# Expert stage of a two-layer encoder: narrow experts on the even partitions, slots spread over all partitions, no remainders on GpSimd, the last k of gate and up multiplied whole in fp32

## The reference, cut to what matters

```python
xt = x.reshape(t, d)                       # t = 1024 tokens, d = 1024
g_idx = argmax of 4 group logits; top_p, top_e = the 2 best of the 8 experts of that group
gate = (g_w[:, None] * top_p).reshape(-1)  # 2048 pairs of token and expert, 32 experts
...
def expert_block(args):                    # for the tokens of one expert
    hid = jax.nn.silu(xe @ w1[e]) * (xe @ w3[e])   # w1, w3: 1024 x 512
    return hid @ w2[e]                             # w2: 512 x 1024
out = jax.ops.segment_sum(yb * buf_gate[:, None], buf_tok, num_segments=t)
```

## Time and profile before

| | us |
|---|---|
| median of 3 runs | 2560.96 (2559.26 to 2565.32) |
| profiled execution | 2557.62 |
| its span | 2555.8 |
| TensorE busy in the span | 2329.6 (91%) |
| VectorE busy | 1884.1 (74%) |
| ScalarE busy | 1474.9 (58%) |
| GpSimd busy | 883.5 (35%) |

### The profile page before, as it was taken

The page is one execution under the profiler, slowest core; times in us unless marked ns, Lnnn a source line. Parts: engine busy times, 40 slices in busy tenths (PEclk is TensorE's granted clock), DMA queues, the critical chain, the costliest instruction groups (busy, mean ns, idle before and its releaser), DMA issues. The chain is left out here.

```text
span 2555.8 us, 33503 instructions
## 1 busy us (share of the span) xinstructions
PE 2329.6 (91%) x11266; PEld 1803.8 (71%) x11266; DVE 1884.1 (74%) x2206; ACT 1474.9 (58%) x1814; POOL 883.5 (35%) x492
## 2 busy tenths in 40 slices
PE   8989999899998899999998999997998899999997
PEld 7768877587876666666666877875886666666664
DVE  7838856678379999899894141478678899899893
ACT  6438842322226888778874241277416777888782
POOL 0001100101003766767660000036003666767662
PEclk9989999999989999999999999998998999999999
DMA  5110001111358999999992031023338999999985
GB/s 182 42 59 2 2 21 66 74 33 38 116 201 337 370 380 375 376 382 379 381 350 81 30 111 67 33 51 116 136 125 349 361 392 387 382 378 374 370 337 208
DMA packets 91932, 540.28 MB, mean 211 GB/s; under 512 B 15596, under 2 KB 27533, under 8 KB 66742
## 3 DMA queue, kind: packets, MB, share of 16 engines
q1 hardware_dynamic: 73926, 499.84, 50.7%
q0 software_dynamic: 15168, 33.59, 5.2%
q10 hardware_dynamic: 2736, 5.51, 0.6%
HBM read 511.58 MB, written 47.22 MB: 219 GB/s over the span
## 5 line engine op out<-in xcount | busy, mean ns | idle before, releaser
L2664 DVE TENSOR_TENSOR wL_rest<-ring,wH 128x2048 fp32r<-128x2048 f32 x162 | 467.4, 2901 | 29.3 <-ACT wH L2563 29.3
L2563 ACT CAST wH<-ring 128x2048 fp32r<-128x2048 f32 x192 | 366.3, 1910 | 76.5 <-PE psum L2397 67.0
L2664 DVE TENSOR_TENSOR wL_rest<-xnT,wH 128x2048 fp32r<-128x2048 f32 x96 | 271.5, 2828 | 35.7 <-ACT wH L2563 35.7
L2389 PE MATMUL psum<-wH,xgH 128*128 128x512 f32 x544 | 221.5, 407 | 54.1 <-DVE xgL L2664 54.1
L2563 ACT CAST wH<-xnT 128x2048 fp32r<-128x2048 f32 x128 | 243.4, 1905 | 15.4 <-PE psum L2397 15.4
L2302 POOL TENSOR_TENSOR wL_rest<-ring,wH 128x2048 fp32r<-128x2048 f32 x30 | 197.9, 6596 | 88.8 <-ACT wH L2563 88.8
L2389 PE MATMUL psum<-wH,hidH 128*128 128x512 f32 (+1 forms) x512 | 207.1, 405 | 22.3 <-DVE hidL L2664 22.3
L2391 PE MATMUL psum<-wH,xgL 128*128 128x512 f32 x544 | 214.4, 394 | 0.0
L2391 PE MATMUL psum<-wH,hidL 128*128 128x512 f32 (+1 forms) x512 | 201.2, 393 | 0.0
L2302 POOL TENSOR_TENSOR wL_rest<-xnT,wH 128x2048 fp32r<-128x2048 f32 x32 | 148.3, 4635 | 129.6 <-ACT wH L2563 129.6
L2389 PEld LDWEIGHTS psum<-wH,xgH 128*128 128x128 f32 x544 | 103.2, 190 | 89.2 <-issue 43.6
(11 more groups left out here) (513 smaller groups left out, 5790.2 us busy)
## 6 DMA issues: line engine op xcount, KB each, us to landing
ring<-in_moe_w SPq DMA_DIRECT2D x92, 2048.0 KB
xnT<-in_moe_w SPq DMA_DIRECT2D x68, 2048.0 KB, 15.4
ow<-in_moe_w SPq DMA_DIRECT2D x34, 2048.0 KB, 14.2
ring<-in_ev_w_in SPq DMA_DIRECT2D x6, 2048.0 KB
ring<-in_od_w_in SPq DMA_DIRECT2D x6, 2048.0 KB
ring<-in_moe_w SPq DMA_DIRECT2D x16, 512.0 KB, 6.0
xn_scratch<-xn_route SPq DMA_DIRECT2D x14, 512.0 KB, 2.6
v_att<-in_x SPq DMA_DIRECT2D x8, 512.0 KB, 4.6
```

Of the source, the lines that this page charges most:

```text
L2389: nc.tensor.matmul(psum[rows, bank, :], xh[:, k, rows], w3[0][:, n, cols], start=(half == 0 and n == 0), stop=False)
L2563: nc.scalar.copy(half_of(wH, i, b, c, half), raw(i, b, c, half)).then_inc(w_high, 1)
L2664: return nc.vector.tensor_tensor(out, whole, high.bitcast(F32), ALU.subtract)
```

## The change

1. Narrow experts no longer use partitions 0 to 63 but the even ones of all 128. Gathers and adds have 128 partitions for every expert; the odd ones of a narrow expert have indices out of bounds. Its tokens are transposed like a wide one's, and the even columns are taken from the result. The table `turn_of_partition` spreads an expert's slots, wide or narrow, over all partitions.
2. GpSimd makes no remainders; VectorE makes all.
3. In the second half of gate and up, the last of the four k is not split: TensorE multiplies it whole in fp32, from the loaded weights and from unsplit tokens (xgW). Cast and remainder of these halves have 1536 columns instead of 2048.
4. The slot of such a tile is freed when TensorE has used it (w_used), since the whole product reads it.

```diff
-    half = np.arange(LESS)
-    turn_of_half = LESS // 4 * (half % 4) + half // 4
-    turn_of_partition = np.concatenate([turn_of_half, LESS + turn_of_half])
+    turn_of_partition = 16 * np.array([0, 4, 2, 6, 1, 5, 3, 7])[np.arange(P) % 8] + np.arange(P) // 8
...
-                def by_gpsimd(i, b, c, half):
-                    return c == 1 and half == 1 and not first(i, b)
+                def in_parts(i, b, c, half):
+                    last_out = isinstance(i, int) and i == PAIRS
+                    return 3 if c < 2 and half == 1 and not last_out else 4
...
                         def freed(i, b, c):
-                            if by_gpsimd(i, b, c, 1):
-                                sp.wait_ge(w_rest, rests(i, b, c, 0))
-                                sp.sem_inc(met, 1)
-                            wait_rest(sp, i, b, c, 1)
+                            if in_parts(i, b, c, 1) < 4:
+                                sp.wait_ge(w_used, after(i, b, c))
+                            else:
+                                sp.wait_ge(w_rest, rests(i, b, c, 1))
...
+                        def whole_product(bank, rows, i, b, c, half, ks):
+                            w = raw(i, b, c, half).rearrange("p (k c) -> p k c", k=len(ks))
+                            nc.tensor.matmul(psum[rows, bank, :], xgW[:, rows], w[:, len(ks) - 1, :],
+                                             start=False, stop=False)
...
-                            wait_rest(pe, i, b, c, half)
+                            if len(split_ks) < len(ks):
+                                whole_product(banks[0], slice(0, P), i, b, c, half, ks)
+                            pe.wait_ge(w_rest, rests(i, b, c, half))
...
-                            last = len(ks) - 1 if half else len(ks)
+                            last = len(split_ks) - 1 if half else len(split_ks)
                             for n in range(last):
                                 both_parts(n, False)
-                            wait_rest(pe, i, b, c, half)
-                            for n, k in enumerate(ks):
+                            if len(split_ks) < len(ks):
+                                whole_product(bank, S, i, b, c, half, ks)
+                            pe.wait_ge(w_rest, rests(i, b, c, half))
+                            for n, k in enumerate(split_ks):
...
-                                if small(i, b) and k == 0:
-                                    nc.tensor.transpose(psum[:, 0, 0:P], xg[:, b, 0:P], ident[:])
-                                elif small(i, b):
-                                    last = nc.tensor.transpose(psum[:, 0, k * LESS:(k + 1) * LESS],
-                                                               xg[S, b, k * P:(k + 1) * P], ident[S, S])
-                                else:
-                                    last = nc.tensor.transpose(psum[:, k // 4, (k % 4) * P:(k % 4 + 1) * P],
-                                                               xg[:, b, k * P:(k + 1) * P], ident[:])
+                                last = nc.tensor.transpose(psum[:, k // 4, (k % 4) * P:(k % 4 + 1) * P],
+                                                           xg[:, b, k * P:(k + 1) * P], ident[:])
...
+                    def even(a):
+                        return a.rearrange("p k (t two) -> p k t two", two=2)[:, :, :, 0]
+                    def even_x():
+                        return even(psum[:, 0:2, :].rearrange("p b (k t) -> p (b k) t", k=4))
...
                                 act.wait_ge(x_hi, e + 1)
-                                nc.scalar.copy(xgH[:, :, S], turned_small(0, KD)).then_inc(xh_ok, 1)
+                                nc.scalar.copy(xgW[:, S], even_x()[:, KD - 1, :])
+                                nc.scalar.copy(xgH[:, :, S], even_x()[:, 0:KD - 1, :]).then_inc(xh_ok, 1)
...
-                            if by_gpsimd(i, b, c, half):
-                                return
+                            cols = slice(0, 512 * in_parts(i, b, c, half))
                             dve.wait_ge(w_high, 2 * chunk(i, b, c) + half + 1)
...
-                                rest(hidL[:, :, S], turned_small(4, 4), hidH[:, :, S]).then_inc(hl_ok, 1)
+                                rest(even(hidL[:]), turned_hid(), even(hidH[:])).then_inc(hl_ok, 1)
```

More of the change, by code:

```diff
@@ L2062, in experts @@
                 idx = sb(st, "gidx" + nm, [P, 2], I32)
-                xgH = sb(st, "xgH" + nm, [P, KD, P], F32R)
-                xgL = sb(st, "xgL" + nm, [P, KD, P], F32R)
+                xgH = sb(st, "xgH" + nm, [P, KD - 1, P], F32R)
+                xgL = sb(st, "xgL" + nm, [P, KD - 1, P], F32R)
+                xgW = sb(st, "xgW" + nm, [P, P])
                 act_h = sb(st, "act_h" + nm, [P, DE])
@@ L2286, in fetch @@
                             e = 2 * i + b
-                            rows = S if small(i, b) else slice(0, P)
                             at = number(rank_of(i, b))
                             pool_e.wait_ge(x_hi, e - 1)
-                            nc.gpsimd.tensor_copy(idx[rows, b:b + 1], slots[rows, bass.ds(at, 1)]).then_inc(idx_ok, 1)
+                            nc.gpsimd.tensor_copy(idx[:, b:b + 1], slots[:, bass.ds(at, 1)]).then_inc(idx_ok, 1)
                             pool_e.wait_ge(idx_ok, e - 1)
@@ L2311, in give @@
                                 pool_e.wait_ge(given, gave + 16 * e)
-                            nc.gpsimd.tensor_copy(yidx[rows, b:b + 1], slots[rows, bass.ds(at, 1)]).then_inc(yidx_ok, 1)
+                            nc.gpsimd.tensor_copy(yidx[:, b:b + 1], slots[:, bass.ds(at, 1)]).then_inc(yidx_ok, 1)
                             pool_e.wait_ge(yidx_ok, e + 1)
@@ L2458, in gate @@
                                 else:
-                                    product((2 + c,), xgH, xgL, i, b, c, half, ks, slice(0, P))
+                                    product((2 + c,), xgH, xgL, i, b, c, half, ks)
                         def out(i, b, at_i, at_b, c):
@@ L2465, in out @@
                             for half in range(2):
-                                product((5, 6), hidH, hidL, at_i, at_b, c, half, range(2 * half, 2 * half + 2),
-                                        S if small(i, b) else slice(0, P))
+                                product((5, 6), hidH, hidL, at_i, at_b, c, half, range(2 * half, 2 * half + 2))
                         def one(i, b):
@@ L2562, in split @@
                                 act.wait_ge(w_used, q - 3)
-                            nc.scalar.copy(half_of(wH, i, b, c, half), raw(i, b, c, half)).then_inc(w_high, 1)
+                            cols = slice(0, 512 * in_parts(i, b, c, half))
+                            nc.scalar.copy(half_of(wH, i, b, c, half)[:, cols], raw(i, b, c, half)[:, cols]
+                                           ).then_inc(w_high, 1)
                         def move_x(i, b):
@@ L2572, in move_x @@
                                 act.wait_ge(turned, e + 1)
-                                nc.scalar.copy(xgH[:, 4 * half:4 * half + 4, :], quarter(half)).then_inc(xh_ok, 1)
+                                if half:
+                                    nc.scalar.copy(xgW[:], quarter(1)[:, 3, :])
+                                n = 4 - half
+                                nc.scalar.copy(xgH[:, 4 * half:4 * half + n, :], quarter(half)[:, 0:n, :]).then_inc(xh_ok, 1)
                         def store_y(i, b, at_i, at_b, c):
@@ L2612, in move_hid @@
                             if small(i, b):
-                                nc.scalar.copy(hidH[:, :, S], turned_small(4, 4)).then_inc(hh_ok, 1)
+                                nc.scalar.copy(even(hidH[:]), turned_hid()).then_inc(hh_ok, 1)
                             else:
@@ L2679, in move_x @@
                                 dve.wait_ge(xh_ok, turned_moves(i, b) + half + 1)
-                                ks = slice(4 * half, 4 * half + 4)
-                                ins = rest(xgL[:, ks, :], quarter(half), xgH[:, ks, :])
+                                n = 4 - half
+                                ks = slice(4 * half, 4 * half + n)
+                                ins = rest(xgL[:, ks, :], quarter(half)[:, 0:n, :], xgH[:, ks, :])
                             ins.then_inc(xl_ok, 1)
```

63 lines of the change are left out of this document (23 added, 40 removed).

## The result

The changed kernel takes 2539.16 us (median of 4, 2534.08 to 2542.4) beside 2560.11 of the kernel before (2556.65 to 2565.32): ratio 0.9915, interval 0.9891 to 0.9939. The forecast was 2542. The profiled execution took 2538.32, its span is 2536.5.

The account below looks back on a forecast made before the run. Bound: a loop of engines waiting for each other, 35.82 us a pair, not the weight stream. Pairs -10.7 and layer starts and ends -8 take 2560.96 to 2542 us; forecast band 2532 to 2552, range 2522 to 2564.

Parts of the forecast that it names:

- The waits: TensorE's three waits in the narrow stage: the first two go, the one for xgL stays at 1.1 us.
- Leg 1: Wide stage, first wide gate product to first narrow one: 18.05 us grows by 0.69 to 18.74.
- +0.25 to +0.3: Narrow expert's transposes on TensorE: eight full-size ones cost this many us more than one full and seven small.
- Leg 2: Narrow stage, first narrow gate product to next wide one: 17.77 us, the next wide gate starting 1.10 earlier.
- I take 0.875: Price in us of each 128x512 fp32 whole product on TensorE, taken from the overflow block's rows.
- Starts and ends of the layers: Outside the steady pairs: -2.5 us at each layer's start, -1.5 at its end, together -8.
- Costed at nothing: GpSimd's gathers and adds on 128 partitions, and strided reads and writes for narrow experts: no cost.
- SP's queue: Weight-load issues: four of six slots freed later, three by about 3 us, without moving the landings.
- the reserve is 24.9 - 16.0 = 8.9 us: Weight slots: 24.9 us from issue to cast, landing at most 16.0, so 8.9 us spare.
- Rival 1: Weight stream is the wall: pace stays near 35.8 us, only layer starts are won, 2556 us; chance 0.16.
- rival 3: More is won: better spread gather rows, TensorE's work the bound, 34.3 us a pair, 2514 us; chance 0.13.
- Rival 2: TensorE dearer: whole products cost 0.38 us more each, +0.73 net a pair, 2572 us; chance 0.15.

Follow-up runs that it names:

- experiments 8 and 9: Narrow whole product on 128 token columns (upper 64 zeros), in the changed kernel: 2531.26 us; in that kernel with VectorE's xgL moved ahead: 2483.38 us.
- Experiment 1: Changed kernel with narrow experts back in partitions 0 to 63 and the old slot table: 2549.62 us, ratio 0.9958.
- experiment 4: Kernel before the change, with one edit: VectorE makes all remainders, GpSimd none: 2528.57 us, ratio 0.9857.
- experiment 10: Changed kernel with VectorE's xgL ahead of gate remainder and multiplication, and narrow experts back in the lower 64 partitions: 2531.95 us, ratio 0.9877.
- experiment 2: Changed kernel without whole products, all k split, slots freed by the remainder: 2517.59 us, ratio 0.9832.
- experiment 3: Changed kernel, but GpSimd again makes the remainder of up's second half, with 1536 columns: 2539.01 us, ratio 0.9912.
- experiment 11: Changed kernel with whole products in wide experts only and VectorE's xgL ahead of gate remainder and multiplication: 2469.8 us, ratio 0.9641.
- experiment 5: Changed kernel without whole products, and with VectorE's xgL of the next expert ahead of gate remainder and multiplication: 2521.76 us, ratio 0.9836.
- experiment 12: Kernel of experiment 11 with VectorE's remainders of the wide halves on 2048 columns, the last 512 unread: 2544.22 us, ratio 0.9919.
- experiment 7: Changed kernel with VectorE's xgL of the next expert ahead of gate remainder and multiplication: 2494.26 us, ratio 0.973.

## Why the prediction was right, and where its steps were not

The time (2542 against 2539.16) and the pace (35.41 against 35.33) came as forecast, in part by luck: errors in the steps cancelled. By its steps:

- *The waits.* Two of three went and xgL's stayed, 1.20 against "stays at 1.1". VectorE took over both remainders at 2.29 and 1.74 us. Right.
- *Leg 1.* Forecast 18.74, measured 18.40. The wide whole products cost what was said (988.73 to 990.29, 1.56 us less 3 x 0.227 = 0.88). The term that was too big is "+0.25 to +0.3" for the narrow expert's transposes: from their start to the next product they take 997.36 - 996.57 = 0.79 us, and before it was 997.72 - 996.94 = 0.78. One full transpose and seven small ones had no smaller price than eight full ones.
- *Leg 2.* Forecast 16.67, measured 16.93. The term that was too small is the narrow whole product, "I take 0.875": 1.16. It was taken from rows with 128 columns of tokens, and 64 cost more (experiments 8 and 9). The one in the narrow gate stands in the chain that ends in xgL: 0.28 us more there, 0.26 in the leg. ScalarE's copy after the narrow gate starts 4.57 us after the gate's first product (1007.48 - 1002.91), 3.87 before, +0.70 where +0.42 was forecast.
- *Starts and ends of the layers.* Forecast -8 in all. Counted from the stage's opening transposes, layer 0's first narrow ones came 3.1 us earlier (815.56 - 759.26 = 56.30 before, 817.34 - 764.14 = 53.20 after; forecast 2.5), and the rest of the stage outside of the pairs gave the remaining 11.3 - 3.1 - 13 x 0.49 = 1.8 (forecast 1.5). Layer 1's -12.8 leaves -6.4 for both (forecast -4). Right in kind, somewhat small. In the profiles the two stages give 24.1 us, not 18.7, and the scatter ahead of layer 0's stage takes 4.9 back.
- *"Costed at nothing".* Strided copies and the wider gathers cost nothing visible: the xL part of a narrow expert takes VectorE 0.62 us (at 998.60), GpSimd's busy time in the window fell to 18.1.
- *SP's queue.* This is the step that failed, though it didn't show in the time. I wrote that landings keep their length and that "the reserve is 24.9 - 16.0 = 8.9 us", which at this pace would do. Experiment 1 is just that case, and the casts ran out of weights at 1138 us. The spread of the rows, which I had put in a rival and given nothing in the sum, kept the time at the forecast: landings fell from 16.0 to about 9, and without it the kernel takes 2549.62. Rival 1's wall is real, at 36.2 to 37.7 us a pair with the old places; rival 3 had the right lever ("rows of a gather are spread better") and the right bound, TensorE, but nothing in this change removes the wait for xgL. The Trainium skill (DMA: Bandwidth & Descriptors, The descriptor swizzle) has engines 0 to 7 write partitions 0 to 63; experiments 1, 4 and 10 agree in their direction, and no row here tells the 16 engines apart.
- *Rival 2,* a dearer TensorE, half came true: 0.28 more on the narrow products, with the wide ones at their price. That the faults of the two legs, -0.34 and +0.26, cancel is luck, and why the pace came out.

What the forecast never asked is what each part is worth alone. Part 2 on the kernel before: -1.43% (experiment 4), more than the change. The spread on top: to -1.68% (experiment 2). Part 3 on top: back to -0.85%. But without part 2 the changed kernel is as fast (experiment 3, -0.88%). Parts 2 and 3 are thus two ways out of the same wait for GpSimd's remainder, and the whole products are the dear one. By the rows they add 2 x 0.20 + 2 x (1.16 - 2 x 0.227) = 1.8 us a pair to TensorE's work, of which 0.83 reaches the pace (34.50 to 35.33). How much of the other 1.0 us is given back by the shorter casts and remainders, and how much falls into time in which TensorE was idle anyway, no run tells; nor is there one with part 1 or part 3 alone on the kernel before. Under the other order the wide half of part 3 turned useful, since it shortens VectorE's row beside which GpSimd issues (experiment 11 against 5 and 12).

Open: why a 64-column fp32 product is dearer than a 128-column one; what decides how long VectorE holds an issue of GpSimd's; and how much of experiment 11's 33.17 us a pair is left in waits for the hidden values.

## What to carry to other kernels

Price the parts of a change one by one against the same chain: here two of three parts removed the same wait, one at no visible cost and one at the price of half the gain, and the third kept the weights in time. Before work is moved off a busy engine, ask whether only its order keeps the critical operand late; moving one small operation forward in the changed kernel was worth 45 us, more than the change itself, though nothing where all k are split (experiment 5). A long unbroken row on VectorE is a hazard for whatever GpSimd issues beside it, even when no engine is seen to wait for VectorE.

## What the runs showed of the hardware

- An fp32 product of 128x512 takes 0.88 us with 128 columns of tokens on the stationary side and 1.16 with 64.
- One transpose of 128 rows and seven of 64 take 0.78 us to the next product, eight of 128 rows 0.79.
- Gathers and adds that fill 64 adjacent partitions go with slower 2 MB loads: at 33.8 us a pair or near it landings grow to almost 30 us (experiment 10), with the rows spread to about 18 (experiment 7). From 850 to 1190 us the core moves 381 GB/s in the one and 402 in the other. With the spread it drew up to 408 over 40 us (experiment 11). The Trainium skill (HBM Reference, Specifications (TRN2)) gives about 425 GB/s for a core that streams alone; the traces stay under that figure, and above the 358 that the prediction had quoted.
- A GpSimd DMA issue of 1.0 to 3.6 us becomes one of 7.5 us (changed kernel), 10.8 (experiment 11, once) or 12.7 to 13.2 (experiments 5 and 12) when it falls on a long row of VectorE's subtractions. It need not: in the kernel before one took 3.06 us inside such a row.
- After TensorE had been idle for 4.02 us its granted clock was 0.58 over the next 6.1 us (experiment 12); in the pairs without such a wait it was 1.00.
